# Sums of squares of the query and key norms: two fp32r passes over a high part and its rest, in place of one fp32 matmul

## The reference, cut to what matters

```python
def rmsnorm(t, g):
    tf = t.astype(jnp.float32)
    return tf * lax.rsqrt(jnp.mean(tf * tf, axis=-1, keepdims=True) + EPS) * g.astype(jnp.float32)
...
qkv = proj[..., o1:o2].reshape(b, l, 3, N_PATTERNS, HEADS_PER_PATTERN, HEAD_DIM)
...
q = rmsnorm(qkv[:, :, 0], q_norm_g[i]) * scale
k = rmsnorm(qkv[:, :, 1], k_norm_g[i])
v = qkv[:, :, 2]
```

## Time and profile before

| | |
|---|---|
| three runs | 2002.28, 2006.12, 2006.95 us; median 2006.12 us |
| profiled execution | 2006.74 us, span 2005.0 us |
| TensorE matmul, busy | 1889.4 us (94%), 8880 instructions |
| GpSimd, busy | 685.3 us (34%) |
| VectorE, busy | 915.0 us (46%) |
| ScalarE, busy | 450.1 us (22%) |
| attention stage | about 67 to 790 us of the span |

### The profile page before, as it was taken

The page is one execution under the profiler, slowest core; times in us unless marked ns, Lnnn a source line. Parts: engine busy times, 40 slices in busy tenths (PEclk is TensorE's granted clock), DMA queues, the critical chain, the costliest instruction groups (busy, mean ns, idle before and its releaser), DMA issues.

```text
span 2005.0 us, 24286 instructions
## 1 busy us (share of the span) xinstructions
PE 1889.4 (94%) x8880; PEld 1486.0 (74%) x8880; DVE 915.0 (46%) x1372; ACT 450.1 (22%) x922; POOL 685.3 (34%) x363
## 2 busy tenths in 40 slices
PE   4799989998998998899899999999999999999999
PEld 2577767776776776778788876788888888788887
DVE  7944564655456469444311222633433333333534
ACT  4233233244323324111311211311111111100000
POOL 6622342334234246664244444121212121122221
PEclk8799989999999999999999999999999999999999
DMA  3031111101111102433421214011111111131211
GB/s 137 32 122 38 42 39 38 52 34 48 38 42 38 32 27 89 117 112 101 158 93 64 94 68 173 33 42 52 42 52 42 52 42 52 52 115 52 84 52 53
DMA packets 50865, 132.68 MB, mean 66 GB/s; under 512 B 9488, under 2 KB 19856, under 8 KB 50656
## 3 DMA queue, kind: packets, MB, share of 16 engines
q1 hardware_dynamic: 38688, 115.71, 16.8%
q10 hardware_dynamic: 11360, 10.03, 1.7%
q0 software_dynamic: 736, 5.86, 0.7%
HBM read 107.82 MB, written 22.58 MB: 65 GB/s over the span
## 4 chain that ended last, share of the span: by engine, by line
PE 72%; DVE 11%; issue 10%; POOL 5%; ACT 1%; DMA 1%; DVEq 0%; SPq 0%; POOLq 0%; ACTq 0%
PE bank L640 21%; PE bank L642 21%; PE bank L641 21%; PE bank L728 2%; PE bank L758 2%; PE bank L785 2%; PE bank L772 2%; DVE run_z L1355 1%; DVE hlo L1297 1%; POOL wlo L483 1%; POOL ssq L614 1%; POOL num L544 1%; DVE zz L1457 1%; DVE run_z L1353 1%; DVE run_n L1340 1%
## 5 line engine op out<-in xcount | busy, mean ns | idle before, releaser
L640 PE MATMUL bank<-hhi,whi 128*128 128x512 f32 x1728 | 707.9, 410 | 52.7 <-POOL wlo L483 29.3
L641 PE MATMUL bank<-hlo,whi 128*128 128x512 f32 x1728 | 690.9, 400 | 0.0
L642 PE MATMUL bank<-hhi,wlo 128*128 128x512 f32 x1728 | 690.7, 400 | 0.0
L483 POOL TENSOR_TENSOR wlo<-raw,whi 128x1024 fp32r<-128x1024 f32 (+1 forms) x146 | 345.9, 2369 | 871.4 <-DVE whi L1206 869.9
L640 PEld LDWEIGHTS bank<-hhi,whi 128*128 128x128 f32 x1728 | 330.9, 192 | 138.7 <-issue 22.7
L642 PEld LDWEIGHTS bank<-hhi,wlo 128*128 128x128 f32 x1728 | 330.9, 191 | 78.6
L641 PEld LDWEIGHTS bank<-hlo,whi 128*128 128x128 f32 x1728 | 331.7, 192 | 71.8 <-issue 0.7
L1206 DVE CAST whi<-raw 128x1024 fp32r<-128x1024 f32 (+1 forms) x146 | 106.1, 727 | 361.1 <-PE bank L642 313.7
L640 PE MATMUL bank<-fhi,whi 128*128 128x512 f32 x352 | 139.7, 397 | 3.0 <-DVE flo L1573 3.0
L641 PE MATMUL bank<-flo,whi 128*128 128x512 f32 x352 | 139.5, 396 | 0.0
L642 PE MATMUL bank<-fhi,wlo 128*128 128x512 f32 x352 | 139.4, 396 | 0.0
(11 more groups left out here) (228 smaller groups left out, 2234.2 us busy)
## 6 DMA issues: line engine op xcount, KB each, us to landing
raw<-in_wblocks SPq DMA_DIRECT2D x138, 512.0 KB, 3.3
rt_scr<-rt POOLq DMA_DIRECT2D x1, 4128.0 KB, 14.1
rt<-rt_scr SPq DMA_DIRECT2D x4, 1032.0 KB, 5.8
x<-in_xT SPq DMA_DIRECT2D x8, 512.0 KB, 7.8
zb_scr<-zb SPq DMA_DIRECT2D x8, 512.0 KB, 3.1
zb<-zb_scr SPq DMA_DIRECT2D x8, 512.0 KB, 3.6
xin<-in_xT SPq DMA_DIRECT2D x8, 512.0 KB, 3.8
x_scr<-x SPq DMA_DIRECT2D x8, 512.0 KB, 6.0
```

Source lines behind the costliest of these rows:

```text
L483: pool.tensor_tensor(wlo[par][:, 0:cols], raw[par][:, 0:cols], whi[par][:, 0:cols].bitcast(F32), ALU.subtract).then_inc(lo_done, 1)
L640: nc.tensor.matmul(ps, a, x, start=start and k == k_list[0], stop=False)
L641: nc.tensor.matmul(ps, a, y, start=False, stop=False)
L642: last = nc.tensor.matmul(ps, b, x, start=False, stop=stop and k == k_list[-1])
```

## The change

blk_ones is also held as fp32r (blkr; ones and zeros), copied once by VectorE at its start. ScalarE copies each sq into an fp32r tile sqh, GpSimd subtracts it from sq into an fp32r tile sql, and TensorE sums both in two fp32r matmuls into the same bank. The DMA scratch of the program is set to 4096 bytes, which makes room for the three new tiles.

```diff
+        blkr = sb("blkr", [P, P], F32R)
+        sqh = sb("sqh", [P, 2, HT], F32R)
+        sql = sb("sql", [P, 2, HT], F32R)
...
 (gpsimd, slot, behind the low half of the weights of steps 0, 4 and 8)
+                    if n is not None and j % 2 and j < 8:
+                        gi = j // 2
+                        pool.wait_ge(sqh_done, 4 * n + gi + 1)
+                        pool.tensor_tensor(sql[:, gi % 2, :], sq[:, gi % 2, :], sqh[:, gi % 2, :].bitcast(F32),
+                                           ALU.subtract).then_inc(sql_done, 1)
                     if n is not None and j in (3, 5, 7, 9):
                         gi = (j - 3) // 2
                         pool.wait_ge(rn_done, 4 * n + gi + 1)
...
 (tensor, slot)
-                        pe.wait_ge(sq_done, 4 * n + gi + 1)
+                        pe.wait_ge(sqh_done, 4 * n + gi + 1)
                         if gi == 0:
+                            pe.wait_ge(blkr_done, 1)
...
-                        nc.tensor.matmul(b_nb[:], blk_ones, sq[:, gi % 2, :], start=True, stop=True).then_inc(ss_done, 1)
+                        nc.tensor.matmul(b_nb[:], blkr[:], sqh[:, gi % 2, :], start=True, stop=False)
+                        pe.wait_ge(sql_done, 4 * n + gi + 1)
+                        nc.tensor.matmul(b_nb[:], blkr[:], sql[:, gi % 2, :], start=False, stop=True).then_inc(ss_done, 1)
...
 (scalar, slot)
                         act.activation(sq[:, gi % 2, :], b_proj[gi % 2][:], ACT.Square).then_inc(sq_done, 1)
+                        act.wait_ge(sq_done, 4 * n + gi + 1)
+                        act.activation(sqh[:, gi % 2, :], sq[:, gi % 2, :], ACT.Copy).then_inc(sqh_done, 1)
...
 (vector, at its start)
+            dve.wait_ge(cst_in, 16)
+            V.tensor_copy(blkr[:], blk_ones).then_inc(blkr_done, 1)
...
-    nc = bacc.Bacc("TRN2", target_bir_lowering=False, num_devices=1)
+    nc = bacc.Bacc("TRN2", target_bir_lowering=False, num_devices=1, dynamic_dma_scratch_size=4096)
```

More of the change, by code:

```diff
@@ L256, in bass_hybrid_block @@
         vt_done, vev_done = sem("vt_done"), sem("vev_done")
+        blkr_done, sqh_done, sql_done = sem("blkr_done"), sem("sqh_done"), sem("sql_done")
         s_done, smx_done, exp_done, t_done, tev, pv_done = (sem(x) for x in ("s_done", "smx_done", "exp_done", "t_done", "tev", "pv_done"))
```

## The result

Six runs of the changed kernel have a median of 2014.38 us (2012.23 to 2016.98), six of the kernel before, on the same chip, 2007.45 (2002.28 to 2008.99). The ratio is 1.0032, 95% interval 1.0020 to 1.0044: slower by 6.4 us, where 2014 was forecast. The profiled execution took 2015.28 us with a span of 2013.6.

What follows compares the result with a forecast made beforehand. TensorE was taken to bound the kernel almost throughout. First slot +4.8, slots 4 +5.2, slots 16 -3.8 and slots 1 -1.9 gave +4.3; with the clock's +3.4, +7.7 on 2006.74, forecast 2014 us, range 2010 to 2018.

Steps and rivals of the forecast that it cites:

- A sum brings at most 0.48 us: On TensorE, two fp32r matmuls and the step behind take 0.47 us instead of 0.95; 48 sums bring at most 23.
- The chain, S+3.06: Square, copy, subtraction and handovers take 2.83 us from the square's start S; what follows the sum can start at S+3.06.
- The copy to hx: Fourth sum, slots 4 and 16: VectorE's copy of exponential sums, held by GpSimd, ends at S+7.95; TensorE 0.6 us later.
- The slots: Attention slots: slots 4 together +5.2 us, slots 16 together -3.8, slots 1 together -1.9.
- The first slot, +4.8: First slot: four subtractions hold up busy VectorE by nearly their whole length, 4 x 1.2 = 4.8 us; bounds 1.2 and 7.
- The clock, +3.4: Long TensorE waits, at the first slot's end and in three slots 4, bring two 1.2 GHz stretches, 1.7 us each.
- the first (VectorE is not held up): VectorE keeps its turn between two GpSimd instructions; first slot costs 1.2, clock nothing: -4.8, 2001 us; chance 0.20.
- the second (all of it is hidden): Added work hides in half-idle ScalarE and GpSimd; all 48 sums gain 0.48: -23, 1983 us; chance 0.06.
- the third: The clock: a slow stretch follows each of four long waits and the first slot costs 7: +13.3, 2019 us; chance 0.14.
- The fifth, 2009 by a cheaper first slot: Gain and loss cancel, the first slot costing 3 and the clock nothing: +2.5, 2009 us; chance 0.13.

Runs made afterwards that it cites:

- the two kernels that split the change: Changed kernel with the old fp32 sum in the first slot only, 2009.19 us; its complement, two passes, copy and subtraction in the first slot only, 2015.06 us.
- The kernel with the work unused: Changed kernel still making copies and subtractions, but TensorE sums sq in full fp32 as before, with one added wait on ScalarE; 2015.72 us.
- the late passes: Changed kernel with both passes of each sum moved behind their step's scores, values and transposes on TensorE; 2001.72 us.

## Why the prediction was right, step by step

- **A sum brings at most 0.48 us.** Too high by a tenth of a microsecond. The 0.23 us between the passes came, but the work behind stands 0.32 to 0.34 behind the second pass and not 0.24, so that two passes and the step take 0.57 and not 0.47. Sums for which TensorE does not wait bring 0.37 to 0.42, where 0.42 to 0.48 was written.
- **The chain, S+3.06.** Met to 0.04, partly by luck: S+3.07 to 3.10 in slots 4 and 16. Where TensorE waits, the second pass starts at S+2.64 and not 2.83, since the handovers to GpSimd and to TensorE are shorter than the ones I took, and what follows stands 0.43 behind it and not 0.23. The two errors cancel. In the second and fourth sum of slot 16 TensorE does not wait at all, and S+3.10 is its own pace. The terms made from the sum of both came well: first sum of slot 4 +1.31 (forecast 1.30), in the last pass S+3.52 instead of S+1.68, +1.84 (1.8); second and fourth sum of slot 1 at S+3.58 (3.62).
- **The copy to hx.** The mechanism was right, turn by turn, the order as written down; the size was not. The copy ended at S+7.43 and not 7.95, L749 stood at S+7.49 and had stood at S+7.41: 0.08 later in slot 16, where I took 0.6 in slots 4 and 16 alike; in slots 4 it is 0.01 to 0.04. The rule that I weighed there, from the Trainium skill, "SBUF — State Buffer", section "SBUF: two separate sides", that the pair is locked for a whole instruction by whoever starts first, agrees with 1.27 us for 0.20. What I mis-sized is the sum of six turns, each some 0.1 us too long, while TensorE had come 2.3 us behind the end of the copy, which now just reaches it.
- **The slots.** Forecast +5.2, -3.8 and -1.9, together -0.5. The change takes a slot 4 of the middle passes from 50.1 to 51.4, +1.3 (forecast 1.69), that of the first pass -0.5 (-0.11), a slot 16 -0.6 (-0.95), a slot 1 -0.6 (-0.62). So slots 4 were charged too much, by the copy to hx, and slots 16 were credited too much, by 0.1 a sum and by what follows. In slot 16 part of the stall that I had charged too high at L749 was paid at the next seam: TensorE is 0.87 ahead at L749 and 0.66 at the transposes of v. The sum is -1.4, with 5 us less at 1.2 GHz; by the two kernels that split the change, nothing measurable. The total is right, by errors that work against each other.
- **The first slot, +4.8.** Right in size, 4.6 (5.6 and 5.8 in two other profiles with these four sums); the transposes at the slot's end start at 108.50, forecast near 109, before 103.89. One part of the story was misplaced: I put new idle time of TensorE of almost 5 us at the slot's end. It is 2.47 there, 2.05 at the third sum and 1.2 at the first, which waits 4.89 behind GpSimd's rotations where the kernel before already stood 3.69. The kernel with the work unused ends the slot 3.3 late without any wait for the subtraction; the rest I put down to that wait.
- **The clock, +3.4.** Too high, and in the wrong places. I expected two more stretches at 1.2 GHz, behind the long waits. Behind the 4.89 us there is one, but the kernel before had one of the same length in that place, behind its own 3.69. Windows, before and after:

```profile
72.50:75.90 3.40, 2.53 (x6) 2.08 (x7) 3.14 (x9) 0.00 (x0) 1.32 (x1) 0.50 0.01 2
```

```profile
75.50:78.90 3.40, 3.40 (x9) 2.63 (x9) 3.09 (x10) 1.57 (x3) 1.72 (x2) 0.50 0.02 7
```

  Behind the waits in slots 4 none came. But a third place has one, and I had not thought of it: the third sum of the first slot. In the profile of the changed kernel TensorE waits 2.05 us there and its clock stays full. In its second profile the wait is 2.90 us, and a stretch of 3.4 us at 1.2 GHz begins near its end:

```profile
87.90 0.80 PE L740 MATMUL bank<-sql,blkr 128*128 128x512 f32 x1 [2.90 <-POOL sql L538]
```

```profile
87.50:90.90 3.40, 3.00 (x7) 2.42 (x8) 3.30 (x5) 1.32 (x2) 2.04 (x2) 0.50 0.40 157
```

  The same is seen with the new sums in the first slot only (2.82 us) and with the late passes (2.50 us), and in none of the seven profiles with the old sum there. In these three the slot ends at 114.4 to 114.7 and not at 113.5. So of the 3.4 about one stretch, at most 1.7 us, has ground in the runs, and not in the places that I named. What is measured is 6.4 to 7.6 us by the ratios, against 4.6 to 5.8 us by the end of the first slot. The 2 between them are as much as the lower mean clock of the changed kernel was estimated to cost, but they also lie within the interval of any one comparison; they stay open.

So the forecast of 2014 was right in sign, in place and in its largest term. In the total it was near partly by luck: the step behind the second pass and the handovers cancelled, slots 4 and slots 16 erred against each other, and the clock's 3.4 stood in for 2 to 3 us that the ratios measure and the stages up to the end of attention do not show.

Of its rivals, the first (VectorE is not held up) falls with the operations of 1.27 us for 0.20 beside a subtraction, the second (all of it is hidden) with the scores of slot 4 at S+3.07, and the third with a first slot that cost 5.8 us at most and three slots 4 with no slow stretch behind their waits. The fifth, 2009 by a cheaper first slot, falls with that slot's 4.6 to 5.8.

## What to carry to other kernels

Splitting an operand to get a cheaper matmul moves the cost to the engines that make the parts: price the chain up to the second part against where the engine's next work stood, and put the consumer behind other work until it fits (here the attention slots took 8.6 us less for moving two matmuls a step). Before giving a short operation to GpSimd because it is idle, look at what VectorE does at that moment: its casts, its copies within SBUF and its two-input operations waited here until a GpSimd instruction had ended (1.27 us for 0.20), so 0.7 us on VectorE was cheaper than 1.3 us on GpSimd although VectorE was the busier of the two. And look for the one stage in which the helper is the bottleneck: four of 48 sums made the whole loss, and leaving these four as they were brought it to zero within 3 us.

## What was not expected of the hardware

- Subtractions and copies for which TensorE never waits cost as much as the whole change (2015.72 us). Beside GpSimd's 48 instructions of 1.36 us VectorE's casts go from 727 to 820 ns in the mean and its 0.2 us operations to 1.27. With the subtraction on VectorE the mean of the casts is back:

```profile
L1215 DVE CAST whi<-raw 128x1024 fp32r<-128x1024 f32 (+1 forms) x146 | 105.5, 723 | 365.8 <-PE bank L646 317.8
```

- The same subtraction takes VectorE 0.69 us and GpSimd 1.29. The Trainium skill, "GPSIMD Engine Reference", section "3.1 Elementwise — side-by-side cycle accounting", has VectorE 1.96 times as fast in an addition of 2048 fp32 elements a partition; these rows, with 512, have 1.87.
- The time at 1.2 GHz in a stretch of unchanged work differs by 14 us between executions of kernels that are the same there. A difference of 0.3% between two single profiles says nothing before this is taken off.
